# Second output projection in two passes over the tokens, with the final norm and residual feature-major

## What is computed

```python
o = swa_prompt_attention(q, k, v, swa_sinks[l])
mp = gated_out(o, gate, swa_w_o[l])        # (o * silu(gate)) @ w_o
...
hp = hp + rmsnorm(mp, post_norm[i])
```

## Time and profile before

| | |
|---|---|
| median of 3 runs | 1806.02 us (1800.91 to 1808.42) |
| the profiled execution | 1804.95 us, of which the span is 1803.2 us |
| busy in the span | PE 1651.0 us, DVE 778.9 us, ACT 547.9 us, POOL 724.4 us |
| mean granted TensorE clock | 0.96 |

### The profile page before, as it was taken

One profiled execution on the slowest core, in us unless ns is written; L12 is line 12 of the kernel. 1 busy time (PEld: TensorE's weight loads), 2 busy tenths in 40 slices (PEclk: granted clock), 3 DMA queues, 4 the chain that ended last, 5 costly groups with the idle time before them and its releaser, 6 DMA issues. The chain is left out here.

```text
span 1803.2 us, 28398 instructions
## 1 busy us (share of the span) xinstructions
PE 1651.0 (92%) x10938; PEld 1542.8 (86%) x10938; DVE 778.9 (43%) x1386; ACT 547.9 (30%) x1162; POOL 724.4 (40%) x872
## 2 busy tenths in 40 slices
PE   6999997899999999999988889994799997998898
PEld 6989997799989999899975589994699997776897
DVE  5126312567575675757653300004744111885013
ACT  5022111344444444444432100002322111773013
POOL 2323322255555555545455123335432131684330
PEclk9999998999999999999998999996999899898899
DMA  4112232011111111112169661104243132541232
GB/s 168 57 47 93 93 111 81 21 63 56 65 57 53 66 57 61 65 46 72 39 213 349 254 237 47 47 29 194 106 152 117 42 111 97 155 123 32 71 117 94
DMA packets 94503, 178.42 MB, mean 99 GB/s; under 512 B 10298, under 2 KB 60235, under 8 KB 94099
## 3 DMA queue, kind: packets, MB, share of 16 engines
q1 hardware_dynamic: 79732, 130.97, 21.3%
q0 software_dynamic: 8448, 24.65, 3.9%
q10 hardware_dynamic: 6208, 21.26, 3.0%
HBM read 129.04 MB, written 49.89 MB: 99 GB/s over the span
## 5 line engine op out<-in xcount | busy, mean ns | idle before, releaser
L606 POOL TENSOR_SCALAR b_prob<-b_prob,b_share 128x896 f32<-128x896 f32 (+7 forms) x128 | 97.0, 759 | 201.8 <-DVE b_share L805 200.0
L1478 DVE TENSOR_TENSOR d_sum<-d_sum,d_sq 128x1032 f32<-128x1032 f32 x14 | 17.3, 1233 | 267.5 <-ACT d_sq L1463 267.5
L129 PE MATMUL ps<-a_xh,w_hi_a 128*128 128x344 f32 x552 | 119.6, 326 | 13.6 <-DVE a_xl L279 10.4
L129 PE MATMUL ps<-a_xl,w_hi_a 128*128 128x344 f32 x552 | 118.1, 323 | 0.0
L706 ACT ACTIVATE b_pth<-ps 128x512 fp32r<-128x512 f32 (+1 forms) x160 | 86.2, 554 | 103.5 <-PE ps L929 93.9
L129 PE MATMUL ps<-a_xh,w_lo_a 128*128 128x344 f32 x552 | 117.4, 321 | 0.0
L129 PE MATMUL ps<-xh,w_hi_f 128*128 128x344 f32 x432 | 93.8, 326 | 25.5 <-DVE xl L1735 20.0
L697 ACT ACTIVATE b_prob<-ps,b_least 128x896 f32<-128x896 f32 (+7 forms) x128 | 94.8, 743 | 58.8 <-DVE b_least L796 57.8
L796 DVE TENSOR_REDUCE b_least<-ps 128x1 f32<-128x896 f32 (+7 forms) x128 | 96.2, 751 | 37.1 <-PE ps L915 36.4
L810 DVE TENSOR_TENSOR b_ptl<-ps,b_pth 128x512 fp32r<-128x512 f32 (+1 forms) x160 | 99.1, 632 | 26.7 <-ACT b_pth L706 25.7
L129 PEld LDWEIGHTS ps<-a_xh,w_hi_a 128*128 128x128 f32 x552 | 93.8, 190 | 15.0 <-issue 10.8
(11 more groups left out here) (302 smaller groups left out, 4574.4 us busy)
## 6 DMA issues: line engine op xcount, KB each, us to landing
c_pages<-in_cache_pages SPq DMA_DIRECT2D x80, 160.0 KB, 4.3
w_raw_a<-in_w_tiles SPq DMA_DIRECT2D x23, 512.0 KB, 3.5
w_raw_f<-in_w_tiles SPq DMA_DIRECT2D x20, 512.0 KB, 3.5
gate_scratch<-a_stage ACTq DMA_DIRECT2D x16, 512.0 KB, 2.6
b_gate<-gate_scratch SPq DMA_DIRECT2D x64, 128.0 KB, 2.5
oh_scratch<-b_oh POOLq DMA_DIRECT2D x64, 128.0 KB, 2.1
ol_scratch<-b_ol POOLq DMA_DIRECT2D x64, 128.0 KB, 2.1
w_raw_d<-in_w_tiles SPq DMA_DIRECT2D x16, 512.0 KB, 3.5
```

Source lines behind the costliest of these rows:

```text
L129: mm = nc.tensor.matmul(ps[:, bank + c, 0:CH], wt, xt[:, k0 + k, c * CH:(c + 1) * CH], start=first and x == 0, stop=last and x == 2)
L606: nc.gpsimd.tensor_scalar(prob[:, n % 4, 0:keys], prob[:, n % 4, 0:keys], share[:, n % 4:n % 4 + 1], 1.0, ALU.mult, ALU.mult).then_inc(nor ...
L1478: nc.vector.tensor_tensor(g.d_sum[:], g.d_sum[:], g.d_sq[:], ALU.add).then_inc(summed, 1)
```

## The change

The matmuls are the same 576, in another order. The 8 weight tiles are split once and stay on chip (`w.hi` and `w.lo` have 8 slots). A first pass of 8 jobs does chunks 0 and 1, 688 tokens (`SPLIT`), into two banks each; a second pass of 8 jobs does chunk 2, 344 tokens, into one bank each. While the second pass runs, the norm and the residual of the first 688 tokens are done feature-major on VectorE, with the inverse root spread over all partitions by a matmul with ones, and stored. Behind the second pass the same is done for the 344 late tokens, with an inverse root taken on 3 columns of tokens, spread by a diagonal and a matmul. The output leaves turned, as `y_turned`, and there are no transposes on the chip; the host turns it back. The loops over jobs are written out. `early` is `g.x_raw`, which lies over `xh`; its columns 0 to 687 are free after the first pass.

The diff, with the removed lines (they stand in the functions above) and the allocations left out:

```diff
@@ phase_last
...
         @block.sync
...
+            for t in range(KT):
+                load_tile(nc, sp, w, a["w_tiles"], B_SO, t // 2, t % 2)
             for k in range(KT):
...
+                nc.sync.dma_start(late[:, k, :], g.h1_dram[k][:, SPLIT:TOK]).then_inc(late_in, 16)
+            sp.wait_ge(w.used, KT)
+            for k in range(KT):
+                nc.sync.dma_start(early[:, k, 0:SPLIT], g.h1_dram[k][:, 0:SPLIT]).then_inc(early_in, 16)
+            for k in range(KT):
+                sp.wait_ge(made_early, k + 1)
+                nc.sync.dma_start(a["y_turned"][k][:, 0:SPLIT], early[:, k, 0:SPLIT]).then_inc(stored, 16)
+            for k in range(KT):
+                sp.wait_ge(made_pool, k + 1) if k < by_pool else sp.wait_ge(made_late, k - by_pool + 1)
+                nc.sync.dma_start(a["y_turned"][k][:, SPLIT:TOK], late[:, k, :]).then_inc(stored, 16)
         @block.gpsimd
...
+            for k in range(by_pool):
+                pool.wait_ge(unit_late, k + 1)
+                pool.wait_ge(late_in, 16 * KT)
+                nc.gpsimd.tensor_tensor(late[:, k, :], late[:, k, :], mt[:, k, SPLIT:TOK], ALU.add).then_inc(made_pool, 1)
         @block.scalar
...
+            for j in range(KT):
+                act.wait_ge(w.used, KT + j + 1)
+                src = ps[:, 4 + j % 2, 0:CH]
+                nc.scalar.activation(sq_late[:, j, :], src, ACT.Square).then_inc(squared_late, 1)
+                keep(j, mt[:, j, SPLIT:TOK], src, read_late)
+                if j == 0:
+                    act.wait_ge(totals_early, 2)
+                    nc.scalar.activation(root[:].rearrange("p (c n) -> p c n", c=2), ps[:, 6:8, 0:CH], ACT.Sqrt,
+                                         scale=1.0 / D, bias=g.eps[:]).then_inc(rooted_early, 1)
+            act.wait_ge(totals_late, 1)
+            nc.scalar.activation(stat[:, 0, :], ps[:, 6, 0:3], ACT.Sqrt, scale=1.0 / D, bias=g.eps[:]).then_inc(rooted_late, 1)
         @block.vector
...
+            dve.wait_ge(rooted_early, 1)
+            nc.vector.reciprocal(root[:], root[:]).then_inc(inverted_early, 1)
+            dve.wait_ge(inverted_early, 1)
+            dve.wait_ge(read_early, KT)
+            dve.wait_ge(early_in, 16 * KT)
+            for k in range(KT):
+                nc.vector.tensor_tensor(mt[:, k, 0:SPLIT], mt[:, k, 0:SPLIT], root[:], ALU.mult).then_inc(unit_early, 1)
+                if k:
+                    dve.wait_ge(unit_early, k)
+                    nc.vector.tensor_tensor(early[:, k - 1, 0:SPLIT], early[:, k - 1, 0:SPLIT], mt[:, k - 1, 0:SPLIT],
+                                            ALU.add).then_inc(made_early, 1)
+                if 2 <= k < KT - 1:
+                    add_late(k - 1)
...
+            add_late(KT - 2)
+            add_late(KT - 1)
+            dve.wait_ge(rooted_late, 1)
+            nc.vector.reciprocal(stat[:, 1, :], stat[:, 0, :]).then_inc(inverted_late, 1)
...
+            nc.vector.tensor_tensor(diag[:], g.ident[:].unsqueeze(1).to_broadcast([P, 3, P]),
+                                    stat[:, 1, :].unsqueeze(2).to_broadcast([P, 3, P]), ALU.mult).then_inc(spaced, 1)
+            dve.wait_ge(replicated, 1)
+            dve.wait_ge(read_late, KT)
+            for k in range(KT):
+                nc.vector.tensor_tensor(mt[:, k, SPLIT:TOK], ps[:, 7, 0:CH], mt[:, k, SPLIT:TOK], ALU.mult).then_inc(unit_late, 1)
+            dve.wait_ge(late_in, 16 * KT)
+            for k in range(by_pool, KT):
+                dve.wait_ge(unit_late, k + 1)
+                nc.vector.tensor_tensor(late[:, k, :], late[:, k, :], mt[:, k, SPLIT:TOK], ALU.add).then_inc(made_late, 1)
         @block.tensor
...
+            for j in range(KT):
+                pe.wait_ge(w.split, j + 1)
+                if j >= 2:
+                    pe.wait_ge(read_early, j - 1)
+                job(j, 2 * (j % 2), (0, 1))
+            for j in range(KT):
+                if j >= 2:
+                    pe.wait_ge(read_late, j - 1)
+                job(j, 4 + j % 2, (2,))
+                if j == 0:
+                    pe.wait_ge(summed_early, KT - 1)
+                    for c in range(2):
+                        nc.tensor.matmul(ps[:, 6 + c, 0:CH], g.ones[:], sum_early[:, c * CH:(c + 1) * CH],
+                                         start=True, stop=True).then_inc(totals_early, 1)
...
+            pe.wait_ge(summed_late, KT - 1)
+            for t, col in enumerate((0, P, CH - P)):
+                mm = nc.tensor.matmul(ps[:, 6, t:t + 1], sum_late[:, col:col + P], g.ones[:, 0:1], start=True, stop=True)
+            mm.then_inc(totals_late, 1)
+            pe.wait_ge(spaced, 1)
+            nc.tensor.matmul(ps[:, 7, 0:2 * P], g.ones[:], diag[:, 0:2, :].rearrange("p t n -> p (t n)"), start=True, stop=True)
+            nc.tensor.matmul(ps[:, 7, 2 * P:CH], g.ones[:], diag[:, 2, 3 * P - CH:P], start=True, stop=True).then_inc(replicated, 1)
```

More of the change, by code:

```diff
@@ L1875, in sem @@
             return st.enter_context(nc.semaphore(name))
[L1877 to L1884, removed]
@@ L1885, in phase_last @@
-        h_turned, m_turned, parted, added = sem("y_h_turned"), sem("y_m_turned"), sem("y_parted"), sem("y_added")
-        stored = [sem(f"y_stored{u}") for u in range(2)]
-        out = out_programs(nc, a, g, w, read, squared, summed_sq, B_SO, g.xh, g.xl, 1, 30, begun=False)
+        w = Weights(nc, st, "h")
+        w.raw = at("w_raw_h", [P, 2, D], 66048)
+        w.hi, w.lo = at("w_hi_h", [P, KT, D], 74240, R32), at("w_lo_h", [P, KT, D], 107008, R32)
+        early = g.x_raw
+        late = at("y_late", [P, KT, CH], 139776)
@@ new lines, in phase_last @@
+        sq_early, sq_late = at("y_sq_early", [P, 2, SPLIT], 150784), at("y_sq_late", [P, KT, CH], 156288)
+        sum_early, sum_late = at("y_sum_early", [P, SPLIT], 167296), at("y_sum_late", [P, CH], 170048)
+        root = at("y_root", [P, SPLIT], 171424)
+        diag = at("y_diag", [P, 3, P], 74240)
+        stat = at("y_stat", [P, 2, 3], 174208)
+        mt = g.mt
+        read_early, read_late = sem("y_read_early"), sem("y_read_late")
+        squared_early, summed_early = sem("y_squared_early"), sem("y_summed_early")
@@ new lines, in phase_last @@
+        squared_late, summed_late = sem("y_squared_late"), sem("y_summed_late")
+        totals_early, rooted_early, inverted_early = sem("y_totals_early"), sem("y_rooted_early"), sem("y_inverted_early")
+        totals_late, rooted_late, inverted_late = sem("y_totals_late"), sem("y_rooted_late"), sem("y_inverted_late")
+        spaced, replicated = sem("y_spaced"), sem("y_replicated")
+        early_in, late_in = sem("y_early_in"), sem("y_late_in")
+        unit_early, made_early = sem("y_unit_early"), sem("y_made_early")
@@ L1888, in phase_last @@
+        unit_late, made_late, made_pool = sem("y_unit_late"), sem("y_made_late"), sem("y_made_pool")
+        stored = sem("y_stored")
+        by_pool = 4
         block = st.enter_context(nc.Block())
-        def tile(t):
-            return (slice(0, P), slice(t * P, (t + 1) * P)) if t < NT else (slice(96, P), slice(TOK - P, TOK))
         @block.sync
         def _(sp):
-            out.sync(sp)
+            for t in range(KT):
+                load_tile(nc, sp, w, a["w_tiles"], B_SO, t // 2, t % 2)
@@ L1906, in _ @@
+            sp.wait_ge(stored, 32 * KT)
         @block.gpsimd
         def _(pool):
-            out.gpsimd(pool)
+            for t in range(KT):
+                pool.wait_ge(w.landed[t % 2], 16 * (t // 2 + 1))
+                nc.gpsimd.tensor_copy(w.hi[:, t, :], w.raw[:, t % 2, :]).then_inc(w.rounded, 1)
+                pool.wait_ge(w.rounded, t + 1)
+                nc.gpsimd.tensor_tensor(w.lo[:, t, :], w.raw[:, t % 2, :], w.hi[:, t, :].bitcast(F32),
+                                        ALU.subtract).then_inc(w.split, 1)
@@ L1916, in _, with keep @@
[L1916 to L1923, removed]
+            def keep(j, own, src, read):
+                nc.scalar.activation(own, src, ACT.Copy, scale=g.gains[:, 30 + j:31 + j]).then_inc(read, 1)
@@ new lines, in _ @@
+            for j in range(KT):
+                u = j % 2
+                act.wait_ge(w.used, j + 1)
+                if j >= 2:
+                    act.wait_ge(summed_early, j - 1)
+                to = sum_early[:] if j == 0 else sq_early[:, u, :]
+                src = ps[:, 2 * u:2 * u + 2, 0:CH]
+                nc.scalar.activation(to.rearrange("p (c n) -> p c n", c=2), src, ACT.Square).then_inc(squared_early, 1)
+                keep(j, mt[:, j, 0:SPLIT].rearrange("p (c n) -> p c n", c=2), src, read_early)
@@ L1925, in _ @@
+            act.wait_ge(totals_late, 1)
+            nc.scalar.activation(stat[:, 0, :], ps[:, 6, 0:3], ACT.Sqrt, scale=1.0 / D, bias=g.eps[:]).then_inc(rooted_late, 1)
         @block.vector
         def _(dve):
[L1927 to L1938, removed]
+            for j in range(1, KT):
+                dve.wait_ge(squared_early, j + 1)
+                if j >= 2:
```

(37 more changed lines are left out.)

8 lines of the change are left out of this document (3 added, 5 removed).

## The result

The changed kernel takes **1789.99 us** (median of 4 runs, 1789.01 to 1791.24), against 1803.99 for the kernel before (median of 4, 1800.91 to 1808.42). The ratio is 0.9921, with a 95% interval of 0.9897 to 0.9945: faster by 0.8%, or 14 us. The profiled execution took 1789.01 us, with a span of 1787.3.

What follows compares the result with a forecast made beforehand. TensorE, busy 92% of the span, was taken as the bound, with the end part behind it also on the path. Replacing 30.5 by 1.3 + 13.8 = 15.1 us gives -15.3 on the median 1806.02: 1790.7 us, range 1784 to 1798.

Steps and rivals of the forecast that it cites:

- 15.3: Whole last phase: forecast saving in us, the path from 1772.74 falling from 30.5 to 15.1, applied to the median 1806.02.
- The matmuls cost nothing more, two added ones 1.3 us: TensorE stream: 0.157 us per matmul stays despite weight changes and single banks; two 344-column sums add 1.3 us.
- T2: End of the second pass on TensorE, forecast at 1774.05 us, which is 1772.74 + 1.3.
- The early work is hidden, with 2.5 us left: VectorE under the second pass: norm and residual of the first 688 tokens end 2.5 us before T2.
- The 0.88 and a hand-over of 0.04: VectorE's early work: 0.88 us for each of 16 operations of 688 columns, and 0.04 for each of 21 hand-overs.
- End part 13.8: From T2 to the end: late tokens' squares, sums, root, spreading, multiplications, additions and store sum to 13.8 us.
- Half rate for the spreading: New end part: TensorE spreads the root at half clock after longer waits; full rate would take some 0.7 us less.
- The end part before, 30.5: Kernel before, from the last matmul at 1772.74 to the span's end at 1803.2: 30.5 us.
- Rival A: Second pass runs at half rate, 0.293 us per matmul: costs 26 us, for 1817; 3%.
- Rival B: Load of `early` takes twice 9.4 us; VectorE ends 4.8 us after T2, for 1795.5; 8%.
- Rival C: Late multiplications: GpSimd and VectorE take turns; GpSimd's four additions add 3.5 us, for 1794; 7%.
- Rival D: Something outside the account, such as instruction supply or bank hand-overs, gives back 7 us or more: about 1800; 6%.

Runs made afterwards that it cites:

- third profiles: Third profiled executions of the kernel before and the changed kernel, unaltered; last phase 120.7 us before and 106.7 us after.
- experiment without cover: Changed kernel, but VectorE starts on the first 688 tokens only after the second pass has ended; 1807.85 us, ratio 1.0026 to the kernel before.
- experiment with 256 late tokens: Changed kernel with 776 early and 256 late tokens, early inverse root on 7 columns, spread by matmuls; 1790.91 us, ratio 0.9916 to the kernel before.
- second profiles: Second profiled executions of the kernel before and the changed kernel, unaltered; last phase 120.7 us before and 107.1 us after.
- experiment with three reciprocals: Changed kernel with VectorE's 688-column reciprocal done three times over under the second pass; one run, 1795.44 us.
- experiment with the root in SBUF: Changed kernel, but ScalarE copies the late tokens' spread root from PSUM to SBUF, where the multiplications read it; one run, 1789.55 us.

## Why the prediction was right

It said 1790.7 us with 1784 to 1798; measured were 1789.99 and, in another set of runs, 1786.18. The mechanism held: the early work went under the second pass, and the end part fell to less than half. That the number came within a microsecond of the first set is partly luck. The 15.3 was taken from a median of three runs, 1806.02, which became 1803.99 with a fourth; from there it gives 1788.7. By its steps:

- *The matmuls cost nothing more, two added ones 1.3 us.* Right: 0.157 each in the second pass at clock 1.00, 1.16 in the chain for the two. T2 was forecast at 1774.05 and came at 1774.43, of which 0.32 is a later start of the phase. That it is so close hides two errors: the half rate at the start, taken as 4.4 us again, lasted 5.8 (some 0.7 us more on the stream), and the stream without that and without the sums came out about 0.5 us shorter than before (both are estimates; the third profiles give the same 0.5). Where the 0.5 comes from is not shown.
- *The early work is hidden, with 2.5 us left.* Hidden, yes; 5.05 were left. The 0.88 and a hand-over of 0.04 for each operation were mis-sized: operations without a fresh wait start 0.79 apart when they last 0.87. The reciprocal of 4.4 was right (4.45), and so was the load, on time. The experiment without cover puts the worth of the hiding at 20 us, more than the whole gain.
- *End part 13.8.* It was 12.9. Multiplications 3.48 for 4.2 (the same mis-sizing), column sums 0.81 for 1.06, spreading 1.34 for 1.55; the store took 2.62, from 1784.68 to the end, for 2.3; four additions 2.29 in the chain, for 2.1 and 0.4 for the meeting.
- *Half rate for the spreading.* Right for all of it in the second and third profile, where the 256 columns took 1.22, and for most of it in the first, where they took 0.96; at the full clock, in the experiment with 256 late tokens, they took 0.71. The reason given was not: the waits of TensorE behind T2 are 1.19 and 1.16 us, each shorter than the 1.51 before, not longer. It waits twice, and has under 1 us of work between.
- *The end part before, 30.5.* This was one execution's value; 28.2 is the commoner in three. By the second profiles the gain is 120.7 - 107.1 = 13.6, by the third ones 14.1, by the first ones 16.2. The sum of 15.3 lies between because it took the end part before at its longest and the new one 0.9 too long: two errors that partly cancel.
- *Rival A* (half rate in the second pass): didn't happen. *Rival B* (VectorE late): no; the experiment with three reciprocals shows where it would begin, 5.05 us on. *Rival C* (turns with GpSimd): one meeting only, the first addition at 1.01 instead of 0.43. The experiment with the root in SBUF shows C's mechanism: 2.9 us on the multiplications, where 3.5 was the rival's price. The Trainium skill ("SBUF — State Buffer", section "SBUF: two separate sides") puts the lock, besides on a perf mode of VectorE with two ports, on VectorE operations with two SBUF inputs, and these only against a GpSimd operation that reads SBUF. This case agrees, 3.48 with an operand in PSUM and 6.36 without. *Rival D*: the gain showed.

## What to carry to other kernels

An end part that can't start before the last sum is cut by the size of the last piece, if the rest can be done under the matmuls of that piece by another engine. Hiding it on the bounding engine gave less than half here: what is hidden takes that engine's own time. Count the cover before relying on it (here 5 us of idle on VectorE), and keep in PSUM an operand that VectorE reads while GpSimd works on SBUF. Where a change is worth less than the scatter of the stages ahead, compare the phase's own length over several profiles, not the span.

## What the runs showed of the hardware that I had not expected

- VectorE's row durations are not its rate: operations of 688 columns last 0.87 us and start 0.79 apart, eight of 344 columns last 0.507 each and together 3.48 (0.43 apart) in the change.
- Whether TensorE's clock falls behind the same wait differs between executions of one program: in the kernel before, behind waits of 1.51 and 1.52 us, it was 0.52 at 1776 to 1778 in one profile, and 1.00 in the other two; that moved the end part by 2.3 us. In the change, with two waits of 1.2 us, it fell in all three profiles, between 2.2 and 3.4 us after the last matmul of the stream.
- How long the phase starts at the half rate differs too, 2.9 to 5.8 us in 13 profiles, and moved the stream of the change by 1.0 us between two of them.
- Stages with the same code ended up to 8.6 us apart in 13 profiles of one core each, with mean clocks of 0.953 to 0.960. The two extremes, 1676.5 and 1685.1, were taken on one and the same chip.
